# Decode attention: score and sparse value products in four 32-row strips instead of two 64-row strips

## What is computed

```python
# A: native sparse attention, 16 heads in 4 key/value groups of 64 columns, three branches
s_c = einsum('bqghd,bcgd->bghqc', q, kc) * scale + bias;  o_c = softmax(s_c) @ vc      # 64 compressed rows
s_s = einsum('bqghd,bgqkd->bghqk', q, kg) * scale + bias; o_s = softmax(s_s) @ vg      # selected blocks of 64
s_w = einsum('bqghd,bkgd->bghqk', q, kw) * scale + bias;  o_w = softmax(s_w) @ vw      # last 512 tokens
o_a = g0 * o_c + g1 * o_s + g2 * o_w
# B: differential attention, 8 heads, two maps of 64 columns each
s1 = einsum('bqhd,bkhd->bhqk', q1, k1) * scale + bias
s2 = einsum('bqhd,bkhd->bhqk', q2, k2) * scale + bias
o_b = rmsnorm((softmax(s1) - lam * softmax(s2)) @ v)                                    # v: 128 columns a head
```

## Time and profile before

| | us |
|---|---|
| median of 3 runs (1842.5 to 1846.8) | 1844.85 |
| the profiled execution | 1843.8 |
| its span, first to last instruction | 1841.9 |
| decode stage, first TensorE product to last | 1013.4 to 1314.8 |
| TensorE matmul busy over the span | 1707.2 |
| VectorE, ScalarE busy over the span | 808.2, 586.6 |

### The profile page before, as it was taken

One profiled execution on the slowest core, in us unless ns is written; L12 is line 12 of the kernel. 1 busy time (PEld: TensorE's weight loads), 2 busy tenths in 40 slices (PEclk: granted clock), 3 DMA queues, 4 the chain that ended last, 5 costly groups with the idle time before them and its releaser, 6 DMA issues. The chain is left out here.

```text
span 1841.9 us, 32875 instructions
## 1 busy us (share of the span) xinstructions
PE 1707.2 (93%) x13036; PEld 1443.1 (78%) x13036; DVE 808.2 (44%) x1866; ACT 586.6 (32%) x1228; POOL 114.6 (6%) x200
## 2 busy tenths in 40 slices
PE   7999999998899987799898999999677999999998
PEld 5888888886788875567776878777476999999998
DVE  4676532104333328777676434434234442234322
ACT  4233211213232326556554222323222331123210
POOL 0000000000000000074122000000010000000000
PEclk9999999988999999989999899999778999999999
DMA  8754444423441316253310789898151234333331
GB/s 284 272 182 150 155 157 145 140 78 73 118 98 30 95 28 189 68 183 106 106 36 12 257 330 313 326 326 340 69 165 46 92 114 122 107 114 114 91 91 49
DMA packets 189947, 265.69 MB, mean 144 GB/s; under 512 B 35310, under 2 KB 119598, under 8 KB 189703
## 3 DMA queue, kind: packets, MB, share of 16 engines
q1 hardware_dynamic: 185710, 244.36, 41.3%
q10 hardware_dynamic: 3096, 11.21, 1.6%
q0 software_dynamic: 1024, 8.59, 1.4%
HBM read 241.04 MB, written 42.60 MB: 154 GB/s over the span
## 5 line engine op out<-in xcount | busy, mean ns | idle before, releaser
L592 PE MATMUL pj_ps<-all_hi,pj_xh 128*128 128x512 f32 x480 | 191.0, 398 | 1.5 <-DVE all_lo L488 1.5
L594 PE MATMUL pj_ps<-all_hi,pj_xl 128*128 128x512 f32 x480 | 189.4, 395 | 0.0
L593 PE MATMUL pj_ps<-all_lo,pj_xh 128*128 128x512 f32 x480 | 189.4, 395 | 0.0
L1382 ACT ACTIVATE pa_sc<-pa_sc,pa_nmax 128x32 f32<-128x32 f32 (+4 forms) x256 | 126.0, 493 | 114.7 <-DVE pa_nmax L1431 114.3
L2512 PE MATMUL fi_ps<-fi_fh,fi_wh 128*128 128x272 f32 x512 | 150.1, 293 | 6.9 <-DVE fi_fl L2440 6.9
L2512 PE MATMUL fi_ps<-fi_th,fi_wh 128*128 128x272 f32 x512 | 149.1, 291 | 1.0 <-DVE fi_tl L2370 1.0
L2513 PE MATMUL fi_ps<-fi_fl,fi_wh 128*128 128x272 f32 x512 | 150.0, 293 | 0.0
L2514 PE MATMUL fi_ps<-fi_fh,fi_wl 128*128 128x272 f32 x512 | 149.7, 292 | 0.0
L2514 PE MATMUL fi_ps<-fi_th,fi_wl 128*128 128x272 f32 x512 | 148.7, 290 | 0.0
L2513 PE MATMUL fi_ps<-fi_tl,fi_wh 128*128 128x272 f32 x512 | 148.0, 289 | 0.0
L1992 ACT ACTIVATE de_slot<-de_ps_t 128x512 f32<-128x512 f32 (+5 forms) x124 | 62.9, 514 | 215.0 <-PE de_ps_t L1832 105.3
(11 more groups left out here) (316 smaller groups left out, 3436.9 us busy)
## 6 DMA issues: line engine op xcount, KB each, us to landing
de_dv<-in_cache_diff SPq DMA_DIRECT2D x64, 512.0 KB, 10.0
all_big<-in_w_in SPq DMA_DIRECT2D x14, 2048.0 KB, 8.4
all_big<-in_cache_nsa SPq DMA_DIRECT2D x96, 256.0 KB, 5.7
de_dk<-in_cache_diff SPq DMA_DIRECT2D x48, 512.0 KB, 9.1
all_big<-in_w_up SPq DMA_DIRECT2D x16, 1024.0 KB, 5.5
all_big<-in_w_down SPq DMA_DIRECT2D x16, 1024.0 KB, 5.5
all_first<-in_cache_nsa SPq DMA_DIRECT2D x32, 256.0 KB
all_win<-in_cache_win SPq DMA_DIRECT2D x32, 256.0 KB, 11.0
```

What stands on the lines that cost most here:

```text
L592: pe.matmul(ps[:, t, 0:width], xh[:, k, xk], hi(k), start=k == 0, stop=False)
L593: pe.matmul(ps[:, t, 0:width], xh[:, k, xk], lo(k), start=False, stop=False)
L594: ins = pe.matmul(ps[:, t, 0:width], xl[:, k, xk], hi(k), start=False, stop=k == KT - 1)
L1382: nc.scalar.activation(tile, tile, ACT.Exp, scale=-1.0, bias=nmax[:, x.n % 6, a:a + 1], accum_out=x.sums[a]).then_inc(probs, 1)
```

## The change

Every score product gets 32 stationary columns and its own 32 rows of PSUM: sequence b and x select rows 64b + 32x. In the sparse mixer x is a pair of key/value groups (128 columns of the keys), and the 32 rows are exactly the heads of these two groups. In the differential mixer the rows are reordered so that strip j of a sequence holds heads 4j to 4j + 3, first map then second; step m now takes heads m and m + 4 in place of 2m and 2m + 1. Nothing is added up over x any more; dif adds up over m = 0 to 3.

The sparse value products are cut to the 128 value columns of two groups: twice as many products of half the width, each into 32 rows. The mask and the reduction on VectorE work on 128 columns instead of 256. `qb` and `qdb` halve. The bias rows of the differential mixer are loaded by 8 DMAs instead of 4, and the queries are laid out by 4 copies instead of 2.

```diff
-N_CONSTS = 10
+N_CONSTS = 14
...
-        for m in range(2):
-            sp.dma_start(a.b_dif[rows.start + 32 * m:rows.start + 32 * m + 32, :],
-                         d["decb"][HEADS:24, :, 0:NCOL].rearrange("h t k -> (h t) k")).then_inc(g.consts_in, 16)
+        for j in range(2):
+            heads = slice(HEADS + 4 * j, HEADS + 4 * j + 4)
+            for m in range(2):
+                at = rows.start + 32 * j + 16 * m
+                sp.dma_start(a.b_dif[at:at + 16, :], d["decb"][heads, :, 0:NCOL].rearrange("h t k -> (h t) k")
+                             ).then_inc(g.consts_in, 16)
...
-        c[r, C_STACK + 32 * b + x % 32] = 1.0
+        c[r, C_STACK + 32 * b + 16 * (x // 32) + x % 16] = 1.0
...
-        c[r, C_MAP + x // 32] = 1.0
-        g = h // HPG
+        c[r, C_MAP + x // 16 % 2] = 1.0
+        g = h // HPG % 2
...
-        qb = s.sb("qb", [P, 2, 2, ROWS])
-        qdb = s.sb("qdb", [P, 2, DHEADS, 2, ROWS])
+        qb = s.sb("qb", [P, 2, 2, 32])
+        qdb = s.sb("qdb", [P, 2, DHEADS, 2, 32])
...
-                            c, h = 2 * b + x, 2 * m + x
+                            c, h = 2 * b + x, m + 4 * x
                             ins = pe.transpose(bank[:, P * c:P * (c + 1)], dk[n % KEY_PAGES][:, b, P * h:P * (h + 1)], ident[:])
...
                     for x in range(2):
                         for b in range(2):
-                            lhs = qdb[:, i % 2, 2 * m + x, b, :] if kind in ("dif", "dif_n") else qb[:, x, b, :]
+                            lhs = qdb[:, i % 2, m + 4 * x, b, :] if kind in ("dif", "dif_n") else qb[:, x, b, :]
+                            rows = slice(ROWS * b + 32 * x, ROWS * b + 32 * x + 32)
                             c = (2 * b + x) * n
                             if kind == "cmp":
                                 c = P * x + CMPS * b
-                            first = x == 0 and m == 0
-                            last = x == 1 and (kind not in ("dif", "dif_n") or m == 3)
-                            ins = pe.matmul(bank[ROWS * b:ROWS * (b + 1), at:at + n], lhs, tile[:, c:c + n],
-                                            start=first, stop=last)
+                            ins = pe.matmul(bank[rows, at:at + n], lhs, tile[:, c:c + n], start=m == 0,
+                                            stop=m == 3 or kind not in ("dif", "dif_n"))
...
-                        for b in range(2):
-                            ins = pe.matmul(ps_n[ROWS * b:ROWS * (b + 1), 0:KVW], tile[:, P * x + ROWS * b:P * x + ROWS * (b + 1)],
-                                            v[:, b, :], start=kind == "p_sel" and k == 0 and x == 0,
-                                            stop=kind == "p_win" and x == 3)
+                        for gp in range(2):
+                            for b in range(2):
+                                o = ROWS * b + 32 * gp
+                                ins = pe.matmul(ps_n[o:o + 32, 0:P], tile[:, P * x + o:P * x + o + 32],
+                                                v[:, b, P * gp:P * (gp + 1)], start=kind == "p_sel" and k == 0 and x == 0,
+                                                stop=kind == "p_win" and x == 3)
...
-                            ins = pe.matmul(ps_n[ROWS * b:ROWS * (b + 1), 0:KVW], tile[rows, P * x + ROWS * b:P * x + ROWS * (b + 1)],
-                                            v, start=False, stop=False)
+                            for gp in range(2):
+                                o = ROWS * b + 32 * gp
+                                ins = pe.matmul(ps_n[o:o + 32, 0:P], tile[rows, P * x + o:P * x + o + 32],
+                                                v[:, P * gp:P * (gp + 1)], start=False, stop=False)
...
                 for m in range(2):
                     half = slice(DD * m, DD * (m + 1))
-                    base = qdb[half, i % 2, 0, 0, 32 * m:32 * m + 1]
...
+                    for j in range(2):
+                        base = qdb[half, i % 2, 4 * j, 0, 16 * m:16 * m + 1]
...
-                    step(nc.vector.tensor_tensor(part[:, 0:KVW], ps_n[:, 0:KVW], con[:, C_NSA:C_NSA + KVW], ALU.mult))
+                    step(nc.vector.tensor_tensor(part[:, 0:P], ps_n[:, 0:P], con[:, C_NSA:C_NSA + P], ALU.mult))
```

More of the change, by code:

```diff
@@ L1526 @@
 CMPS = ROWS
-C_GROUP, C_STACK, C_IDX, C_WIN, C_MAP, C_NSA, C_DIFF = 0, 128, 192, 209, 213, 215, 471
-C_ALL = 983
+C_GROUP, C_STACK, C_IDX, C_WIN, C_MAP, C_NSA, C_DIFF = 0, 128, 192, 209, 213, 215, 343
+C_ALL = 855
 def decode_constants():
@@ L1818, in turn @@
                             c = 2 * b + x
-                            ins = pe.transpose(bank[:, DEC_T * c:DEC_T * (c + 1)],
-                                               src[:, b, P * (2 * m + x):P * (2 * m + x + 1)], ident[one, one])
+                            h = m + 4 * x if kind == "dif_n" else x
+                            ins = pe.transpose(bank[:, DEC_T * c:DEC_T * (c + 1)], src[:, b, P * h:P * (h + 1)], ident[one, one])
                 elif kind == "cmp":
@@ L2069, in lay_queries @@
                     for g2 in range(2):
-                        half, x = slice(DK * g2, DK * (g2 + 1)), 2 * gp + g2
+                        half = slice(DK * g2, DK * (g2 + 1))
                         ins = nc.vector.tensor_copy(
-                            qb[half, gp, :, 16 * x:16 * (x + 1)].rearrange("p b (h t) -> p h b t", t=DEC_T),
+                            qb[half, gp, :, 16 * g2:16 * (g2 + 1)].rearrange("p b (h t) -> p h b t", t=DEC_T),
                             ps_n[half, Q_AT + 32 * gp:Q_AT + 32 * (gp + 1)].rearrange("p (h b t) -> p h b t", h=HPG, t=DEC_T))
@@ L2079, in lay_diff_queries @@
                     half = slice(DD * m, DD * (m + 1))
-                    base = qdb[half, i % 2, 0, 0, 32 * m:32 * m + 1]
-                    out = bass.AP(tensor=base.tensor, offset=base.offset,
-                                  ap=[list(base.ap[0]), [2 * ROWS + DEC_T, DHEADS], [ROWS, 2], [1, DEC_T]])
-                    ins = nc.vector.tensor_copy(out, ps_n[half, Q_AT + 64:Q_AT + 128].rearrange("p (h b t) -> p h b t", h=DHEADS, t=DEC_T))
+                    for j in range(2):
+                        base = qdb[half, i % 2, 4 * j, 0, 16 * m:16 * m + 1]
+                        out = bass.AP(tensor=base.tensor, offset=base.offset,
+                                      ap=[list(base.ap[0]), [2 * 32 + DEC_T, 4], [32, 2], [1, DEC_T]])
+                        at = Q_AT + 64 + 32 * j
+                        ins = nc.vector.tensor_copy(out, ps_n[half, at:at + 32].rearrange("p (h b t) -> p h b t", h=4, t=DEC_T))
                 ins.then_inc(qdb_ready, 1)
@@ L2160, in _ @@
                         dve.wait_ge(nsa_stored, 32 * i)
-                    nc.vector.tensor_reduce(o_n[:], part[:, 0:KVW].rearrange("p (g e) -> p e g", e=DK), AX.X, ALU.add).then_inc(nsa_out, 1)
+                    nc.vector.tensor_reduce(o_n[:], part[:, 0:P].rearrange("p (g e) -> p e g", e=DK), AX.X, ALU.add).then_inc(nsa_out, 1)
                     dve.wait_ge(nsa_out, i + 1)
```

## The result

In twelve runs each, side by side, the kernel before took 1846.07 us (median) and the changed kernel 1830.27. The ratio, taken over all the runs and so not quite that of the two medians, is 0.9906, 95% interval 0.9878 to 0.9933: faster, by 12 to 23 us. The forecast was 1822, with a range of 1805 to 1837. A second comparison of the same two kernels (`after_again`) gave 1846.72 and 1831.13, ratio 0.9883 (0.9832 to 0.9935). Of all the runs in this document one was a slow one, more than 1.5% above the fastest of its kernel (scores_only, 1850.21), and the ratios leave it out.

The account below looks back on a forecast made before the run. TensorE was taken as the bound, with DMA a close second that would become the next limit. 1843.8 us less 26.9 (19.7 up to the last pair, 7.2 in it) plus 5 for the clock gave 1822, range 1805 to 1837.

Parts of the forecast that it names:

- The arithmetic of four strips: Decode score and value products: score phase from 1.02 to 0.59 us, 13.5 us a pair, 54 in all if TensorE stays bound.
- no overlap: Rival: strips of one bank or the sequencer hold the four products apart, phases stay 1.02, time 1844; chance 0.06.
- The small steps: Decode steps of 4 new keys: half the bursts, 0.21 us gained per 2 steps, with cmp 0.8 per pair.
- Pages, not TensorE, bound next: Decode: after the change TensorE waits 6 to 9 us a pair for key pages; T0 to T0 66.7 us.
- 1790: Rival total in us: TensorE keeps the whole 54 us gain; chance 0.06.
- T0: End of p_dif_n in a pair; from here SyncE issues value pages and key pages 4 and 5, said to need 27.4 us.
- Why page 7 comes when it does: Decode loads: T1's loads queue behind T0's 27.4 us and take 17 more (13.5 good end, 20.6 bad) until key page 7.
- T1: End of p_win in a pair; from here SyncE issues the next pair's selected pages and key pages 6 and 7.
- The copies: Decode: two more tiny query copies on VectorE a pair, +0.4 us, priced at nothing as covered by dense TensorE work.
- the window that the prediction named and dismissed: Where branches are chosen: VectorE busy 8.1, ScalarE 5.9 of 10 us, dismissed since before T1 TensorE has 6 us to spare.
- The coefficients: Last pair, chain from last scores over the exponential to p_dif's coefficients: 1.4 us of the gain lost.
- The clock: Decode: half clock after page waits of about four us costs 1.7 us in three of four pairs, 5 us; ends 0 and 26.

Follow-up runs that it names:

- scores_only: The changed kernel with the sparse value products put back to 64 rows and 256 columns; 1832.36 us, ratio 0.9904 to before.
- short_v_after: The changed kernel loading only 256 of 1024 columns of each differential value page in pairs 1 to 3; 1817.6 us (one run).
- fill: The changed kernel with 20 extra identity transposes on TensorE before the wait for key pages 6 and 7, pairs 0 to 2; 1823.88 us, ratio 0.9859.
- values_later: The changed kernel with key pages 6 and 7 issued ahead of selected pages, and value pages moved further back; 1807.47 us, ratio 0.9787.
- table_early: The changed kernel with SyncE reading the next pair's page numbers earlier; in pair 0 value pages 4 and 5 go behind key page 7; 1822.62 us, ratio 0.9883.
- keys_first: The changed kernel with SyncE issuing key page 6 before the next pair's selected pages, page 7 before pages 3 to 7; 1809.6 us, ratio 0.9772.

## Why the prediction was right, and where not

**The arithmetic of four strips** held: 0.58 for 0.59, p_sel's gain 1.72 for 1.7, the whole pair 13.3 to 14.3 for 13.5. So the rival *no overlap* is out: 16 records within 0.58 us are 36 ns each. The Trainium skill's 62 ns per matmul ("TensorE: Matmul & The Clock Gate", section "Wait — 56ns, not 53.3ns?") is stated there for hardware decode off; it does not bind here, and no run shows which setting this chip had. The small steps were undersized: 16 records of a dif_n now take 0.23 from start to start, where those of the earlier trace rows took 0.56 (1110.57 to 1111.13), a gain of 0.33 for 0.21.

**Pages, not TensorE, bound next**: right, and it is what kept the forecast from 1790. The waits are 5.8 and 4.4 us in pairs 1 and 2, a little under the 6 to 9 forecast, and T0 to page 7 is 45.4 for 44.4.

**Why page 7 comes when it does** was the step that failed, though its number nearly fit: "T0's loads need 27.4, T1's queue behind them, take 17". The landing of T0's batch at 27.1 was right, but it hardly sets page 7. Cutting it to 19.3 (short_v_after) left page 7 at T1 + 21, and brought it 2.3 us sooner, not 8. The chain of pair 1 is SyncE's: T0 to the end of the last value issue 14.5, reading the table 9.6, 22 issues up to page 7's last 12.5, its landing 8.8, then TensorE's 23.6 to T0: 69.0. In pair 2, where the reading is not late, it runs over T1: T0 to T1 23.0, first issue 0.2, the 22 issues 13.3, landing 8.6, then 23.8: 68.9. So in both the term that was missing is T1, or SyncE's readiness, plus some 21 to 22 us of issues and landing. The prediction had seen T1 + 20.6 and used it only as the bad end of a range; it had not asked what SyncE does between its last issue and T1, 11.9 us in which no row stands. In pair 0, where SyncE was latest, page 7 came at T1 + 28.1, for 20.0 before.

**The copies**, priced at nothing, cost 4.0 us on VectorE and 0.4 on ScalarE. VectorE's timeline, pair 1: the copy for the new keys' scores (L2110) stands behind the branch's masks and row maxima (L2024), as it did before, and TensorE now comes for it sooner:

```profile
1109.51 1.23 DVE L2024 CUSTOM_DVE_ANT_1 de_s_sel<-de_s_sel,de_pick 128x1024 f32<-128x1024 f32 x1 [0.19 <-DVE de_pick L2143]
...
1111.30 0.69 DVE L2024 CUSTOM_DVE_ANT_0 de_s_win<-de_ps_s,all_b_win 128x512 f32<-128x512 f32 x1
...
1112.11 1.36 DVE L2110 COPY de_slot<-de_ps_t 128x16 f32<-128x16 f32 x3
```

It is 0.9 to 1.4 us in each of pairs 1 to 3, in pair 1 in the window that the prediction named and dismissed. By the rows the dismissal was half right: the waits make T1 later, but in pairs 0 and 1 SyncE is later still. No run took them away. The coefficients in the last pair cost 1.3 for 1.4.

**The clock** was undersized: 5 us forecast, ends 0 and 26. TensorE was busy 30.9 us at half clock, a loss of 15.5, where before it was 1.7; 2.7 come back at decode's start, with 7.9 us at half clock for 13.2. Net 11. Part of it is hidden, since a slow stretch between pages 6 and 7 only shortens the wait for page 7; fill puts what shows at 1.5 us after page 7. Nor is all of it the doing of the page waits: the stretch at 1208.7 began ahead of its wait. The last part lost the most: 6.8 us at half clock, all busy, after a wait of 1.3. That loss of 3.4 is most of the difference between its 58.2 and the forecast 54.4; scores_only, with none there, took 56.3, and values_later, once with none and with other loads, 53.7.

The balance of the decode stage: -54 (four strips), +18.1 (page waits, 20.8 for 2.7), +4.4 (copies), +1.3 (coefficients), +11.1 (clock) is -19.1; measured -20.9. The forecast's 27.1 of waits were 23.8, and its 5 of clock 11: two errors against each other, so that the stage came out within 1 us of the forecast is in part luck. What stays open is the rest of the total: the forecast took 21.9 us off, and the medians differ by 15.8 us, and no run tells these 5 to 6 us apart from the variation of other stages.

## What to carry to other kernels

When an engine's work is cut, write the chain of the runner-up from one of its own gates to the next, issue by issue, and ask of each gap in a queue's rows what the sequencer does there: register reads leave no row and are free only until the engine they feed is early. Here a transfer's place in its queue was worth 3.9 us of the stage while TensorE was slow and 14.5 once it was fast, beside the 20.9 of the change itself, so try the order of the loads together with such a change. And two halves of a change that each gain alone need not add up once another resource ends last.

## What the hardware showed that was not expected

- Reading 16 page numbers on SyncE took 9.2 to 9.6 us, some 0.6 each, during which it issued nothing. The load after it moved when the reading did (table_early, pair 1: first issue at T1 + 0.2 for 2.2 and 1.9).
- Half clock came after waits as short as 0.9 us (after_again, 1115.8, then 3.4 us from 1116.0), while the same wait in the changed kernel's first profile (1112.33) had none behind it, nor had 2.73 us in keys_first, before 1203.46, or 2.03 us before. The wait of 1.3 us for the coefficients brought 6.8 us in the changed kernel and none in values_later. The length of a single wait does not tell whether the clock falls. The Trainium skill, in "TensorE: Matmul & The Clock Gate", section "Why this matters for your kernels", warns of idle gaps between bursts; here each of the six page waits of 1.8 to 4.3 us in pairs 0 to 2 of the changed kernel had half clock behind or around it, though one of these stretches began ahead of its wait.
- Extra work of no use in place of waiting did not make the stage longer: 278.3 us, for 280.9 and 283.2 in the two profiles without it, which differ by as much between themselves.
